# The down product of the prompt's rows as seven block products, with sums of w_down made by GpSimd during the gates

## The chip, the core and the metric

The kernel runs on one core of a Trainium2 chip. A core has five engines with an instruction stream each: TensorE (PE, matrix products), VectorE (DVE), ScalarE (ACT), GpSimd (POOL) and SyncE (SP, which here only issues transfers). They meet through semaphores. Transfers go through 16 DMA engines that all streams share. The metric is device time in microseconds; the kernel before took 1920.28 us, the median of 3 runs (1920.12 to 1924.04).

## The reference, cut to what matters

The reference is one layer of a decoder for 1024 prompt rows and 64 sample rows (8 sequences with 8 new tokens each), so 1088 rows of width 1024, in float32.

```
z = rmsnorm(x, norm1_g) @ w_in            # 1024 -> 5120: queries, keys, values (3072) and two gates (2048)
gate = sigmoid(g + b_gate)                # 16 tiles of 128 channels, "the gates"
m = gate[0] * (o_a @ w_proj_a) + gate[1] * (o_b @ w_proj_b)
x = x + m @ w_o
u = rmsnorm(x, norm2_g) @ w_up            # 1024 -> 5632, then a causal convolution of width 3
f = gelu(a) * b                           # a, b: the two halves, 2816 channels each = 22 tiles of 128
y = rmsnorm(x + f @ w_down, norm_f_g)     # the down product: 2816 -> 1024
```

Outputs are y for all rows and the new key, value and convolution caches; most of the cache output is a shifted copy of an input (`cache3` is 8 x 4 MB).

## The kernel before

All large products are float32 products made of three passes: each operand is split into a head (its value rounded to the multiplier's format, made by ACT) and a rest (made by DVE), and TensorE adds head x head, head x rest and rest x head.

The work is in stages, one after the other, with the order of each engine written out by hand; no planner decides anything. Only semaphores tie the engines, and each engine takes its own list strictly in order. Three stages are touched.

The front stage (`front_stage`, up to about 490 us) makes z in six column blocks of 512, and then the gates, in 8 units of two channel tiles. A unit is a Strassen-Winograd product: four block products' worth of matrices are combined so that seven block products P1 to P7 of 24 matmuls (128x272 each) do instead of eight. Its weights arrive by `load_unit` (line 330, 1 MB, issued by POOL) in one of two buffers `raw_g0`, `raw_g1`; ACT makes the heads (`unit_head`, line 415), DVE the rests (`unit_rest`, line 598) and the four sums S1 to S4 of the weights. `load_unit(s)` waits until every rest of unit s - 2 is made (`lo_made`). POOL also issues `copy_cache` (line 333), eight copies of 4 MB from HBM to HBM: four of them beside the loads of z's blocks, one right after `load_unit(0)`, three in the gates.

The tail stage (`tail_stage`, from about 997 us) makes m, x and then u: three channel tiles plainly and 19 in units like those of the gates (from 1233 to 1635 us). There the four weight sums of a unit are made by POOL (`sum_s3`, `sum_s2`, `sum_s1`, `sum_s4`, lines 2369, 2374, 2380, 2385), which also stores each finished tile of f to HBM (`store`, line 2389). The convolution runs on DVE (lines 2728 and 2733).

The down product (from 1635 us) goes through the nine row tiles in three trios (`TRIOS`). Each trio takes 22 steps, one for each channel tile k: SP loads 128 rows of w_down (512 KB) and the trio's part of f (192 KB), ACT and DVE split both, and PE does `down(n)`, 18 matmuls of 128x512 (16 in the last trio, whose sample tile needs fewer). Two buffers of each kind are in use, so a step's load can be at most two steps ahead. As step 4 is reached, x (4.3 MB) is loaded back (lines 2350 and 2351). Finished banks are added to x by DVE (`add_out`, lines 2784 and 2786), followed by the square, the root and the scaling (`scale_out`, line 2798) of the final norm, and SP stores y.

## Time and profile before

| | |
|---|---|
| time, median of 3 | 1920.28 us |
| the profiled execution | 1921.66 us, its span 1920.0 us |
| PE busy | 1787.1 us (93%), 12290 matmuls |
| DVE, ACT, POOL busy | 1131.9, 794.1, 251.3 us |
| granted TensorE clock, mean | 0.966 of full speed |
| the down product's matmuls (line 3070) | 1144, 263.4 us busy |
| HBM traffic | 283 MB read, 96 MB written |

How to read it: the profile is one execution. An engine's busy time says little by itself, since each stage has another limit; what counts is in which stretches PE stands still or runs at a lower clock, and what it waits for there. The rows below are from the windows (busy time by stretch), the timelines of single engines (start, duration, what ended the idle time before), the groups of instructions and the list of transfers.

### The profile page before, as it was taken

To read this page: it belongs to the slowest core of one execution; us is meant where nothing else is said; L and a number is where in the kernel's file an instruction comes from. 1 tells how busy PE (TensorE), PEld (TensorE's weight loads), DVE (VectorE), ACT (ScalarE), POOL (GpSimd) and SP (SyncE) were. 2 spreads that over 40 slices of the span, in tenths; PEclk is the share of its full clock that TensorE was granted. 3 is DMA by queue.
4 is the path that set the end of the run, shared out by engine and by line. 5 is a ranking of instruction groups with operands and counts; after the bars stand their busy time and mean duration, and the time that the engine had idled before them with its cause. 6 is when DMAs were issued, how large, how long until landed. Compare 5 with 4: busy or idle time off the path is not lost. (4 is left out here: it accounts for less than half of the span.)

```text
span 1920.0 us, 32200 instructions
## 1 busy us (share of the span) xinstructions
PE 1787.1 (93%) x12290; PEld 1526.8 (80%) x12290; DVE 1131.9 (59%) x1935; ACT 794.1 (41%) x1479; POOL 251.3 (13%) x321
## 2 busy tenths in 40 slices
PE   7999999899778887999988999999999999899997
PEld 6777779899545555666668889999999999788875
DVE  5224575343364787666667368667777776445455
ACT  4220014343673576333332134455555554334343
POOL 0000000000100301232300002133223222000000
PEclk9999999999978789999989999999999999999998
DMA  6444535732711936999956435132232222756664
GB/s 232 173 178 178 215 121 183 263 111 72 194 29 42 323 120 229 392 386 389 385 187 216 148 116 180 48 90 68 68 95 75 68 70 86 249 177 203 190 209 139
DMA packets 169826, 331.13 MB, mean 172 GB/s; under 512 B 35769, under 2 KB 97098, under 8 KB 167306
## 3 DMA queue, kind: packets, MB, share of 16 engines
q1 hardware_dynamic: 143242, 193.58, 30.8%
q0 software_dynamic: 26432, 135.50, 19.4%
q8 instruction: 98, 1.61, 0.3%
q14 instruction: 54, 0.44, 0.1%
HBM read 283.02 MB, written 95.68 MB: 197 GB/s over the span
## 5 line engine op out<-in xcount | busy, mean ns | idle before, releaser
L3070 PE MATMUL tl_ps<-tl_dn,tl_f 128*128 128x512 f32 x1144 | 263.4, 392 | 8.5 <-DVE tl_f L2771 6.9
L3070 PEld LDWEIGHTS tl_ps<-tl_dn,tl_f 128*128 128x128 f32 x1144 | 216.1, 189 | 55.5 <-DVE tl_dn L2767 8.9
L3004 PE MATMUL tl_ps<-tl_T_hi,tl_slots 128*128 128x272 f32 x1216 | 211.5, 288 | 1.2 <-ACT tl_u L2456 1.2
L3004 PEld LDWEIGHTS tl_ps<-tl_T_hi,tl_slots 128*128 128x128 f32 x1216 | 175.4, 188 | 1.5 <-ACT tl_u L2456 1.5
L3004 PE MATMUL tl_ps<-tl_X_hi,tl_slots 128*128 128x272 f32 x912 | 161.1, 288 | 0.7 <-ACT tl_u L2525 0.7
L2767 DVE TENSOR_TENSOR tl_dn<-all_lead,tl_dn 128x1024 fp32r<-128x1024 f32 x66 | 80.9, 1225 | 136.5 <-ACT tl_dn L2534 136.5
L766 PE MATMUL fr_ps<-fr_w_hi,h_hi 128*128 128x512 f32 x384 | 152.7, 398 | 2.4 <-DVE h_lo L550 2.4
L766 PE MATMUL fr_ps<-fr_w_lo,h_hi 128*128 128x512 f32 x384 | 152.1, 396 | 0.0
L766 PE MATMUL fr_ps<-fr_w_hi,h_lo 128*128 128x512 f32 x384 | 150.3, 391 | 0.0
L2534 ACT ACTIVATE tl_dn<-all_lead 128x1024 fp32r<-128x1024 f32 x66 | 70.0, 1060 | 160.4 <-PE tl_ps L3070 132.7
L3004 PEld LDWEIGHTS tl_ps<-tl_X_hi,tl_slots 128*128 128x128 f32 x912 | 132.2, 188 | 0.9 <-ACT tl_u L2525 0.9
L2728 DVE SCALAR_TENSOR_TENSOR tl_c<-tl_u,tl_cw,tl_c 128x1023 f32<-128x1023 f32 x88 | 121.2, 1378 | 15.1 <-ACT tl_c L2473 13.5
L3004 PE MATMUL tl_ps<-tl_T_lo,tl_slots 128*128 128x272 f32 x608 | 125.5, 288 | 0.0
L3004 PEld LDWEIGHTS tl_ps<-tl_T_lo,tl_slots 128*128 128x128 f32 x608 | 95.8, 189 | 0.0
L3004 PE MATMUL tl_ps<-tl_X_lo,tl_slots 128*128 128x272 f32 x456 | 94.1, 288 | 0.0
L766 PEld LDWEIGHTS fr_ps<-fr_w_hi,h_hi 128*128 128x128 f32 x384 | 72.6, 189 | 21.1 <-DVE h_lo L550 2.8
L766 PEld LDWEIGHTS fr_ps<-fr_w_hi,h_lo 128*128 128x128 f32 x384 | 72.7, 189 | 16.2
L766 PEld LDWEIGHTS fr_ps<-fr_w_lo,h_hi 128*128 128x128 f32 x384 | 72.8, 190 | 14.4
L778 PE MATMUL fr_ps<-h_hi,fr_slots 128*128 128x272 f32 x480 | 83.0, 287 | 0.0
L778 PE MATMUL fr_ps<-fr_X_hi,fr_slots 128*128 128x272 f32 x384 | 69.1, 292 | 8.0 <-DVE fr_slots L598 7.3
L2473 ACT ACTIVATE tl_c<-tl_u,tl_cb,tl_cw 128x1088 f32<-128x1088 f32 x44 | 57.1, 1298 | 47.0 <-DVE tl_u L2756 46.2
L2743 DVE TENSOR_TENSOR tl_slots<-all_lead,tl_slots 128x512 fp32r<-128x512 f32 x70 | 62.4, 904 | 23.5 <-ACT tl_slots L2505 23.1
(384 smaller groups left out, 3734.4 us busy)
## 6 DMA issues: line engine op xcount, KB each, us to landing
all_lead<-in_w_down SPq DMA_DIRECT2D x66, 512.0 KB, 3.6
out_s<-in_cache POOLq DMA_DIRECT2D x8, 4080.0 KB, 20.6
pg_pages<-in_pool POOLq DMA_DIRECT2D x64, 256.0 KB, 6.3
pg_pages<-in_pool SPq DMA_DIRECT2D x64, 256.0 KB, 7.2
pg_odds<-in_pool SPq DMA_DIRECT2D x64, 256.0 KB, 7.9
all_lead<-in_w_up SPq DMA_DIRECT2D x26, 512.0 KB, 5.1
zs<-fr_zt SPq DMA_DIRECT2D x48, 256.0 KB, 2.0
fd<-tl_c POOLq DMA_DIRECT2D x22, 544.0 KB, 4.9
```

The costliest lines, as they stand in the source:

```text
L766: last = pe.matmul(zbank[at % 3], h[:, k, c0:c0 + P], w[:, k, :], start=(m == 0), stop=(m == 3 * KD - 1))
L778: last = pe.matmul(ps[:, (bank + n) * 512:(bank + n) * 512 + SIDE // 2], w[:, k, :], h[:, k, n * SIDE // 2:(n + 1) * SIDE // 2], start=(fi ...
L2473: act.activation(c[:, i, :], row, ACT.Identity, bias=cb[:, t:t + 1], scale=cw[:, 2, t:t + 1]).then_inc(scaled, 1)
L2534: act.activation(dn[n % 2][:, 0, :], dn_raw[:, n % 2, :], ACT.Copy).then_inc(dn_hi_done, 1)
L2728: dve.scalar_tensor_tensor(out=x, in0=row[:, p0:p1 - back_by], scalar=cw[:, tap_of, t:t + 1], in1=x, op0=ALU.mult, op1=ALU.add).then_inc(t ...
L2743: dve.tensor_tensor(slots[:, SLOT_OF[name], 1, :, :], weights(s_, name), slots[:, SLOT_OF[name], 0, :, :].bitcast(F32), ALU.subtract).then ...
L2767: dve.tensor_tensor(x[:, 1, :], dn_raw[:, n % 2, :], x[:, 0, :].bitcast(F32), ALU.subtract).then_inc(dn_lo_done, 1)
L3004: last = pe.matmul(ps[:, (bank + n) * 512:(bank + n) * 512 + SIDE // 2], w[:, k, :], h[:, k, n * SIDE // 2:(n + 1) * SIDE // 2], start=(fi ...
L3070: last = pe.matmul(down_bank(m), x, w[:, h * 512:h * 512 + 512], start=(k == 0 and q == 0), stop=(k == FT - 1 and q == len(passes) - 1), s ...
```

## The change

Three edits, in two stages.

First, the down product of the 1024 prompt rows becomes a Strassen-Winograd product. The 22 channel tiles are halved into 11 and 11, the rows into 512 and 512, and the 1024 output columns into 512 and 512. Seven products P1, P6, P2, P5, P3, P7, P4 come one after the other (`DOWN`), each over 11 channel tiles (`FH`), with 4 row tiles times 3 passes = 12 matmuls of 128x512 in a step. A step now loads two pieces of 256 KB: a block of f or of its sums (`sd`), and a block of w_down or of its sums (`td`). Raw steps go through 4 buffers and split steps through a ring of 11. The 64 sample rows are multiplied plainly beside P1, P2, P5 and P3 (two matmuls for each channel tile and column half). In the last product the four row tiles are finished one after the other (`last_down`), each followed by its own norm and store.

Second, the sums. POOL makes those of w_down in the front stage: 22 parts, each with two loads, four additions of 128x256 and a store to `td`, with two buffers. They stand in POOL's list between the `load_unit` calls, four parts ahead of each of units 3 to 7. POOL makes the sums of f in the tail stage as the tiles are finished (`difference`, `add_sums`). The weight sums of the 19 units, which POOL made before, move to DVE.

Third, `copy_cache`: all eight copies are now issued beside the loads of z's blocks, two for each of blocks 2 to 5; none is left in the gates.

```diff
@@ front_stage, POOL @@
                 load(p)
-                copy_cache(p - 2)
-            pool.wait_ge(xn_ready, RT)
+                copy_cache(2 * p - 4)
+                pool.wait_ge(z_ready, (p - 1) * RT + 5)
+                copy_cache(2 * p - 3)
             load_unit(0)
-            copy_cache(NZ - 2)
...
             load_unit(1)
-            copy_cache(NZ - 1)
-            for s_ in range(2, NU):
-                pool.wait_ge(lo_made, 7 * (s_ - 1))
-                load_unit(s_)
-                if s_ < 4:
-                    copy_cache(NZ - 2 + s_)
+            def load_part(i):
+                if i >= 2:
+                    pool.wait_ge(wsum_stored[i % 2], 16 * (i // 2))
+                for q in range(2):
+                    pool.dma_start(wsum[:, i % 2, q, :, :], w_parts[i // 2, i % 2, q]).then_inc(wsum_in[i % 2], 16)
+            def sum_part(i):
+                x = wsum[:, i % 2, :, :, :]
+                pool.wait_ge(wsum_in[i % 2], 32 * (i // 2 + 1))
+                pool.tensor_tensor(x[:, 1, 1, :], x[:, 1, 1, :], x[:, 0, 1, :], ALU.subtract).then_inc(wsum_step, 1)
...
+                pool.wait_ge(wsum_step, 4 * i + 4)
+                pool.dma_start(td[i // 2, :, :, (i % 2) * 256:(i % 2) * 256 + 256],
+                               x.rearrange("p q n c -> p (q n) c")).then_inc(wsum_stored[i % 2], 16)
+            pool.wait_ge(lo_made, 7)
+            load_unit(2)
+            pool.wait_ge(t_lo_done, 3)
+            load_part(0)
+            for i in range(2 * FH):
+                if i + 1 < 2 * FH:
+                    load_part(i + 1)
+                sum_part(i)
+                if i % 4 == 3 and 3 + i // 4 < NU:
+                    pool.wait_ge(lo_made, 7 * (2 + i // 4))
+                    load_unit(3 + i // 4)
@@ tail_stage @@
+        DOWN = ("P1", "P6", "P2", "P5", "P3", "P7", "P4")
+        STEPS = len(DOWN) * FH
+        LEAD = 5
...
@@ SP @@
             for n in range(STEPS):
                 if n == 4:
+                    sp.wait_ge(tap, 8 * (FT - 1))
+                    sp.wait_ge(beside, 8 * (FT - 1))
+                    load_samples(0)
                     sp.wait_ge(p_ready, made("P3", UNITS - 1, UNITS))
                     sp.dma_start(x2[:, 0:QT, :], ...).then_inc(x2_back, 16)
...
@@ POOL, for each tile j of f from the 12th on @@
+            def add_sums(j):
...
+                pool.tensor_tensor(sums[:, 0, :], c[:, 1, HALF2], sums[:, 0, :], ALU.subtract).then_inc(sum_step, 1)
+                pool.tensor_tensor(sums[:, 1, :], c[:, 1, HALF2], sums[:, 1, :], ALU.add).then_inc(sum_step, 1)
...
+                pool.tensor_tensor(s4[:, :], c[:, 1, HALF1], sums[:, 0, :], ALU.subtract).then_inc(sum_step, 1)
@@ DVE, units and down product @@
                     rest(s_ + 1, "S3")
+                    sum_s2(s_ + 1)
                     rest(s_ + 1, "S2")
+                    sum_s1(s_ + 1)
                     rest(s_ + 1, "S1")
+                    sum_s4(s_ + 1)
...
+                q, after = divmod(n - FH - LEAD, FH)
+                if q >= 0 and after == 0:
+                    for at in range(4):
...
+                                add_out(DOWN[q], at, quarter)
...
+            for at in range(4):
+                add_out("P4", at, (1, 0))
+                finish(1 + at)
@@ PE @@
+            def row_tile(n, q, r):
+                k, (hi, lo) = n % FH, (ring[n % FH][:, part, :] for part in range(2))
+                for m, (x, w) in enumerate(three_passes(hi[:, r * P:r * P + P], lo[:, r * P:r * P + P], hi[:, 512:1024], lo[:, 512:1024])):
+                    last = pe.matmul(down_bank(4 * q + r), x, w, start=(k == 0 and m == 0), stop=(k == FH - 1 and m == 2))
...
+            def last_down():
+                q = len(DOWN) - 1
+                for r in range(4):
+                    bank_free(4 * q + r)
+                    for k in range(FH):
+                        if r == 0:
+                            pe.wait_ge(step_lo, q * FH + k + 1)
+                        row_tile(q * FH + k, q, r)
```

POOL's list in the gates, before: loads of units (`fr_raw_g`) and copies (`out_s3`), each load behind DVE's rests.

```order
L330 DMA fr_raw_g1<-in_w_in 128x8x256 [waits fr_z_stored1,fr_z_stored2,fr_z_stored0,fr_z_ready]
L333 DMA out_s3<-in_cache3 64x16320
L330 DMA fr_raw_g0<-in_w_in 128x8x256 [waits fr_lo_made]
L333 DMA out_s3<-in_cache3 64x16320
L330 DMA fr_raw_g1<-in_w_in 128x8x256 [waits fr_lo_made]
```

The same place in the changed kernel, from one part's loads to the next unit's load; three more such parts stand between the load of unit 2 and this one, and four between any two later unit loads.

```order
L362 DMA fr_wsum<-in_w_down 128x2x256 [waits fr_wsum_stored0]
L362 DMA fr_wsum<-in_w_down 128x2x256
L368 TENSOR_TENSOR fr_wsum<-fr_wsum 128x256 [waits fr_wsum_in1]
L370 TENSOR_TENSOR fr_wsum<-fr_wsum 128x256 [waits fr_wsum_step]
L372 TENSOR_TENSOR fr_wsum<-fr_wsum 128x256 [waits fr_wsum_step]
L374 TENSOR_TENSOR fr_wsum<-fr_wsum 128x256 [waits fr_wsum_step]
L376 DMA td<-fr_wsum 512x1x256 [waits fr_wsum_step]
L334 DMA fr_raw_g1<-in_w_in 128x8x256 [waits fr_lo_made]
```

The copies have gone from here, and a unit's load now stands behind additions and behind waits for stores of the sums.

DVE's list in one unit of the tail, before: rests (`tl_slots`) and the first half of the convolution.

```order
L2762 TENSOR_TENSOR tl_u1<-tl_u1,tl_ps 128x544
L2743 TENSOR_TENSOR tl_slots<-tl_raw1,tl_slots 128x512 x4
L2728 SCALAR_TENSOR_TENSOR tl_c<-tl_u1,tl_cw,tl_c 128x1023
L2733 SCALAR_TENSOR_TENSOR tl_c<-tl_ue,tl_cw,tl_c 128x2x32
L2728 SCALAR_TENSOR_TENSOR tl_c<-tl_u1,tl_cw,tl_c 128x1022
```

The same unit in the changed kernel, with the sums (`tl_raw1<-tl_raw1`) between the rests.

```order
L2885 TENSOR_TENSOR tl_u1<-tl_u1,tl_ps 128x544
L2845 TENSOR_TENSOR tl_slots<-tl_raw1,tl_slots 128x512 x2
L2856 TENSOR_TENSOR tl_raw1<-tl_raw1 128x4x128
L2845 TENSOR_TENSOR tl_slots<-tl_raw1,tl_slots 128x512
L2862 TENSOR_TENSOR tl_raw1<-tl_raw1 128x4x128
L2845 TENSOR_TENSOR tl_slots<-tl_raw1,tl_slots 128x512
L2867 TENSOR_TENSOR tl_raw1<-tl_raw1 128x4x128
L2830 SCALAR_TENSOR_TENSOR tl_c<-tl_u1,tl_cw,tl_c 128x1023
```

The rests and the convolution keep their order; three sums stand among them, and the fourth (`sum_s3`) ahead of the unit's last product.

## Rows read from the trace of the kernel before

**Rows 1.** Windows: stretch; busy PE, PEld, DVE, ACT, POOL; clock, DMA share, GB/s
```profile
100.00:200.00 100.00, 100.00 (x469) 80.04 (x468) 38.84 (x59) 13.53 (x8) 2.86 (x4) 1.00 0.47 173
340.00:360.00 20.00, 18.94 (x152) 18.73 (x151) 3.24 (x6) 2.29 (x4) 1.14 (x2) 1.00 0.96 352
360.00:380.00 20.00, 13.79 (x97) 13.82 (x98) 8.61 (x14) 8.32 (x13) 0.90 (x1) 0.83 0.53 172
1300.00:1400.00 100.00, 100.00 (x799) 100.00 (x799) 73.42 (x93) 51.34 (x101) 27.73 (x22) 1.00 0.27 82
1650.00:1660.00 10.00, 3.10 (x10) 2.26 (x9) 2.26 (x3) 3.05 (x4) 0.00 (x0) 0.83 0.82 274
```

**Rows 2.** Timeline of POOL in the gates: start, duration, instruction, idle before
```profile
322.84 0.90 POOL L330 DMA_DIRECT2D fr_raw_g<-in_w_in  x1 [7.23 <-DVE fr_slots L598]
...
339.71 0.90 POOL L330 DMA_DIRECT2D fr_raw_g<-in_w_in  x1 [15.45 <-DVE fr_slots L598]
...
371.90 0.90 POOL L330 DMA_DIRECT2D fr_raw_g<-in_w_in  x1 [30.75 <-DVE fr_slots L598]
...
411.71 0.88 POOL L330 DMA_DIRECT2D fr_raw_g<-in_w_in  x1 [20.07 <-DVE fr_slots L598]
432.67 0.88 POOL L330 DMA_DIRECT2D fr_raw_g<-in_w_in  x1 [20.07 <-DVE fr_slots L598]
```

**Rows 3.** Timeline of ACT in the gates
```profile
364.20 0.62 ACT L423 ACTIVATE fr_even_u<-fr_ps 128x544 f32<-128x544 f32 x1 [15.50 <-DMA gs<-fr_even_u]
...
388.11 0.61 ACT L415 ACTIVATE fr_slots<-fr_raw_g 128x512 fp32r<-128x512 f32 x1
392.08 0.63 ACT L427 ACTIVATE held_rows<-fr_ps 128x544 f32<-128x544 f32 x1 [3.36 <-PE fr_ps L778]
...
454.94 0.63 ACT L427 ACTIVATE fr_even_u<-fr_ps 128x544 f32<-128x544 f32 x1 [3.35 <-PE fr_ps L778]
```

**Rows 4.** Groups on POOL: instruction, shapes, count; busy us, mean ns; idle before
```profile
L2385 POOL TENSOR_TENSOR all_lead<-all_lead 128x512 f32<-128x512 f32 x10 | 17.4, 1737 | 0.0
...
L2374 POOL TENSOR_TENSOR all_lead<-all_lead 128x512 f32<-128x512 f32 x10 | 12.8, 1279 | 34.7 <-DVE tl_slots L2743 34.7
...
L952 POOL DMA_DIRECT2D pd_krow<-zs x7 | 5.0, 723 | 69.3 <-POOLq L141 59.9 <-PE pd_tbank L1134 9.3
```

**Rows 5.** Transfers issued by POOL: count, KB each, median us to landing
```profile
out_s<-in_cache POOLq DMA_DIRECT2D x8, 4080.0 KB, 20.6
...
fd<-tl_c POOLq DMA_DIRECT2D x22, 544.0 KB, 4.9
...
fr_raw_g<-in_w_in POOLq DMA_DIRECT2D x8, 1024.0 KB, 7.1
...
x2d<-tl_x POOLq DMA_DIRECT2D x8, 512.0 KB, 2.9
```

**Rows 6.** Group: the matmuls of the down product
```profile
L3070 PE MATMUL tl_ps<-tl_dn,tl_f 128*128 128x512 f32 x1144 | 263.4, 392 | 8.5 <-DVE tl_f L2771 6.9 <-DVE tl_f L2774 0.8 <-DVE tl_x L2786 0.6
```

**Rows 7.** Timeline of all engines, last trio of the down product and the end
```profile
1887.91 0.33 SPq L2298 DMA_DIRECT2D all_lead<-in_w_down  x1
...
1891.54 0.33 SPq L2298 DMA_DIRECT2D all_lead<-in_w_down  x1
...
1903.57 0.69 DVE L2784 TENSOR_TENSOR tl_x<-tl_x,tl_ps 64x512 f32<-64x512 f32 x1 [1.23 <-PE tl_ps L3070]
...
1914.09 1.28 DVE L2798 SCALAR_TENSOR_TENSOR tl_y<-tl_x,tl_rstd,tl_gain_f 128x1024 f32<-128x1024 f32 x1
```

**Rows 8.** The chain that ended last, start of the down product: start, us, what
```profile
1642.42 14.51 DMA tl_f_raw<-fd
```

**Rows 9.** Timeline of DVE in one unit of the tail
```profile
1417.96 0.72 DVE L2762 TENSOR_TENSOR tl_u<-tl_u,tl_ps 128x544 f32<-128x544 f32 x1 [2.53 <-ACT tl_u L2525]
1418.60 1.29 DVE L2743 TENSOR_TENSOR tl_slots<-tl_raw,tl_slots 128x512 fp32r<-128x512 f32 x2
1422.00 1.17 DVE L2743 TENSOR_TENSOR tl_slots<-tl_raw,tl_slots 128x512 fp32r<-128x512 f32 x1 [2.11 <-ACT tl_slots L2505]
```

More of the change, by code:

```diff
@@ L55 @@
 UNITS = FT - PLAIN_UP
+FH = FT // 2
 def rows_of(t):
@@ L2122, in _, with tail_stage @@
             turn_out_shared(NB - 1)
-def tail_stage(nc, K, a, o, zs, gs, early, x2d, fd):
+def tail_stage(nc, K, a, o, zs, gs, early, x2d, fd, sd, td):
     with stage(nc, "tl") as s:
@@ L2229, in bank_pair, with sample_bank, added_before @@
+        def sample_bank(i):
+            return ps[:, S_BANKS[i] * 512:S_BANKS[i] * 512 + 512]
+        def added_before(name, r, quarter):
+            before = [ADDED[what] for what in ADDS[:ADDED[(name, r, quarter)] - 1] if what[1:] == (r, quarter)]
+            return max(before, default=0)
         def bank_pair(b):
@@ new lines, in load_step, with load_samples @@
+                if name in ("P1", "P2", "P3"):
+                    r0, c0 = (0 if name == "P1" else FH) + k, 512 if name == "P3" else 0
+                    sp.dma_start(to[:, 512:1024], a["w_down"][r0 * P:r0 * P + P, c0:c0 + 512]).then_inc(landed, 16)
+                else:
+                    sp.dma_start(to[:, 512:1024], td[k, :, ("P6", "P5", "P4", "P7").index(name), :]).then_inc(landed, 16)
+            def load_samples(i):
+                for s_ in range(2):
+                    c0 = s_ * (ROWS - SROWS // 2)
+                    sp.dma_start(fs_raw[:, :, s_ * SROWS // 2:(s_ + 1) * SROWS // 2],
+                                 fd[i * FH:(i + 1) * FH, :, c0:c0 + SROWS // 2].rearrange("k p r -> p k r")).then_inc(fs_in, 16)
@@ L2633, in _ @@
             for n in range(4, STEPS):
[L2634 to L2639 removed]
+                step_head(n)
+                if n == 4:
+                    sample_heads(0)
+                if n == FH + 3:
+                    sample_heads(1)
+                if n == FH + LEAD:
+                    for at in range(4):
+                        keep(at)
+                if 0 <= n - 5 * FH - LEAD - 1 < FIRST:
+                    final_square(n - 5 * FH - LEAD - 1)
+                if n == 5 * FH + LEAD + 7:
+                    final_root(0)
+            for g in range(1, len(NORMS)):
                 for i in range(*NORMS[g]):
@@ L2888, in _ @@
             rest(1, "A11")
+            sum_s3(1)
             for s_ in range(UNITS):
@@ new lines, in row_tile, with samples_part @@
+            def row_tile(n, q, r):
+                k, (hi, lo) = n % FH, (ring[n % FH][:, part, :] for part in range(2))
+                for m, (x, w) in enumerate(three_passes(hi[:, r * P:r * P + P], lo[:, r * P:r * P + P], hi[:, 512:1024], lo[:, 512:1024])):
+                    last = pe.matmul(down_bank(4 * q + r), x, w, start=(k == 0 and m == 0), stop=(k == FH - 1 and m == 2))
+                if k == FH - 1:
+                    last.then_inc(out_ready, 1)
+                return last
+            def samples_part(n, half, side, first, final):
+                k, (hi, lo) = n % FH, (ring[n % FH][:, part, 512:1024] for part in range(2))
+                pe.wait_ge(fs_lo_done, half + 1)
+                for m, w in enumerate((hi, lo)):
+                    last = pe.matmul(sample_bank(side), fs[half][:, k, :], w, start=(first and k == 0 and m == 0),
+                                     stop=(final and k == FH - 1 and m == 1))
+                if final and k == FH - 1:
+                    last.then_inc(s_ready, 1)
+                return last
@@ new lines, in first_samples, with down @@
+            def first_samples(k):
+                if k == 0:
+                    pe.wait_ge(c21_done, UNITS)
+                samples_part(k, 0, 0, True, False)
+                samples_part(k, 0, 1, True, False).then_inc(d_done, 1)
+            def down(q):
+                name = DOWN[q]
+                for k in range(FH):
+                    n = q * FH + k
+                    pe.wait_ge(step_lo, n + 1)
+                    if name == "P2":
+                        samples_part(n, 1, 0, False, True)
+                    if name == "P5":
+                        samples_part(n, 0, 1, False, False)
+                    if name == "P3":
+                        samples_part(n, 1, 1, False, True)
+                    for r in range(4):
+                        if k == 0:
+                            bank_free(4 * q + r)
+                        last = row_tile(n, q, r)
+                    if q and k < FH - 1:
+                        last.then_inc(d_done, 1)
+                    if q == 0 and k >= 4:
+                        first_samples(k - 4)
+                if q == 0:
+                    for k in range(FH - 4, FH):
+                        first_samples(k)
@@ L3116, in _ @@
                     p7(s_ + 1)
-            for n in range(STEPS):
-                down(n)
+            for q in range(len(DOWN) - 1):
+                down(q)
+            last_down()
 def program(nc, a, o, scratch):
```

411 lines of the change are left out of this document (232 added, 179 removed).

## The prediction

> **What bounds the kernel now.** I read the windows first, stretch by stretch, because the three edits lie in three stages. In the blocks of z, PE is busy for the whole stretch although one 4 MB copy runs beside each block: 100 of 100 us, DMA share 0.47 [rows 1]. In the units of the tail PE is again busy for 100 of 100 us, while DVE stands at 73 and POOL at 28 [rows 1]. So z and the units are bound by PE, and there an edit on another engine only matters if it comes to the path. Two stretches are not like that. From 340 to 380 us PE is busy for 32.7 of 40 us, and in the second half its granted clock is 0.83 [rows 1]. The timeline of POOL shows the same place: unit loads, which otherwise follow each other at 20.96 us (432.67 - 411.71), are 32.2 us apart there (371.90 - 339.71) [rows 2]. ACT tells why: it stood 15.5 us for a store of the gates that was late [rows 3], while the copies of the cache, 20.6 us each [rows 5], held the DMA engines (share 0.96). That stall costs 11.2 us, of which 7.3 are idle and 3.9 are work at the lower clock. The second place is the start of the down product: 3.1 of 10 us busy at 1650 us [rows 1]. There a step's load took 14.5 us behind the 4.3 MB of x [rows 8]. Elsewhere the down product is PE-bound: 8.5 us idle before 1144 matmuls [rows 6], and 16 matmuls every 3.63 us in the last trio, 0.227 us each [rows 7].
>
> **The down product.** The new one has 7 x 11 x 12 = 924 matmuls for the prompt and 4 x 11 x 2 = 88 for the samples, 1012 in place of 1144, all 128x512. 132 fewer at 0.227 us are **-30.0 us**. Feeding them is not the limit: a step is 12 matmuls, 2.7 us, and needs one head and one rest of 128x1024 and 512 KB, and the ring reaches 11 steps ahead where two buffers did before. Three places are left.
>
> At the start the load of x stands again ahead of step 4's load in SP's list. x and step 4 land about where x and step 4's load landed before (14.5 us after issue, [rows 8]); head and rest take some 2.3 us more, so step 4 is ready near 1655 us. The four steps ready by then are 10.9 us of work instead of 16.3, with step 3 late by some 2 us behind the convolution. That makes some 9.5 us of idle where before had 8.5 [rows 6]: **+1**. It could be +6 if the 2816 small pieces of the sample rows are slow, and 0 at best.
>
> At the last product all 11 steps are wanted within the first row tile, one each 0.68 us. DVE makes the rests of five of them only after the eight additions for P7, at about 0.7 us each, that it stands in at P7's end. The eleventh is ready about 9.7 us after that end, where PE wants it after 6.8: **+2.9**. Bounds 0 and 6. For the changes of banks at the other products I take **+1**: PE has 6 matmuls of the next product, 1.4 us, before it needs a bank that DVE has just freed.
>
> At the end, 17.7 us lie between PE's last matmul (1903.57 - 1.23) and the end of the span [rows 7]. Six additions of 0.69 us become one, and two scalings of 1.28 us and a square leave the chain, because each row tile is now finished by itself while PE is at the next: **-7** (bounds -4 and -9).
>
> The down product in sum: -30 + 1 + 2.9 + 1 - 7 = **-32 us**.
>
> **The units.** Four sums of 128x512 come to DVE, at the 0.645 us that a rest takes in quiet [rows 9]: 2.6 us of a 21 us unit. Two things cover them. DVE stands 2.5 us before its first subtraction and 2.1 us before a rest, where it waits for ACT's head of a sum that POOL took 1.28 us for [rows 4, 9]; DVE makes that sum in half the time, so the chain S2, head, rest, S1, head, rest gets no longer. And the rest in [rows 9] that took 1.17 us beside POOL's additions would take 0.65 alone. I take **0**; if the cover fails, DVE is late by up to 1 us a unit, 19 us in all, and the sums of f on POOL (three additions of 128x512 a tile) are far from filling 21 us.
>
> **The copies.** Moved beside z's blocks they run one at a time, half a block apart. The stretch of 100 us in [rows 1] held two loads and two copies (the 4 instructions on POOL) with PE at 100 of 100; it will hold four copies of 20.6 us each [rows 5], 82 of 100 us. I take 0 there. In the gates the stall of 11.2 us goes. What is late next is not PE but POOL.
>
> **The sums of w_down.** Here the change adds waits to the list that feeds the gates. In a part, POOL waits for the store of the part before (only two buffers, and that store was issued just ahead), issues two loads, makes four additions, each behind the one before, and issues the next store. So the landing of the store lies bare in every part. The period:
> - store from issue to landing: 2.9 us for 512 KB of x2d when all is quiet, 4.9 for 544 KB of fd beside loads [rows 5]. The new one goes out in pieces of 1 KB, beside the gates' stores; I take 3.4, nearer to the size and the quiet.
> - two load issues at 0.72 us: 1.4 [rows 4].
> - four additions of 128x256: half of 1.28 (quiet) to half of 1.74 (beside DVE) [rows 4]; I take 0.75, which makes 3.0. No row has the short form.
> - semaphores between them, 0.3.
>
> That is **8.1 us a part**, bounds 7.2 (2.9 + 1.4 + 2.6 + 0.3) and 10.1 (4.9 + 1.4 + 3.5 + 0.3). Four parts stand ahead of each unit's load: 32 us, where PE takes 20.96 us a unit. Queued behind the waiting part is the unit's load, and ACT waits for it: the head of a unit's A11 (L415 at 388.11) stands in ACT's list ahead of `keep_u2` (L427 at 392.08, 3.4 us after ACT fell idle [rows 3]), and PE's P7 waits for that one. So unit 7's weights must have landed by 454.94 - 0.63 = 454.3 us to cost nothing. They land as follows. Unit 2's load goes at 322.84 [rows 2] and takes 7.1 us [rows 5]; part 0 lands behind it, near 331.3. The 20th part ends 19 periods, four additions (3.3) and a store issue (0.7) later, and the load takes 7.1 us more: 331.3 + 19 x 8.1 + 11.1 = 496.3 us. Late by **42 us**, net of the stall that goes, since 454.3 is measured with that stall in it. After each wait PE starts at a lower clock, as it did after 360 us; before the last wait this hides in the next one, but the 30 us of PE work after it pay once: **+4**.
>
> In the Trainium skill, "GPSIMD Engine Reference", the section on elementwise work side by side, gives 2.6 cycles an element for a two-input addition at 1.2 GHz, 0.56 us for 256 elements, and calls VectorE the place for such work. The trace shows more, 1.28 us for 512 in quiet. By the page the period is 7.3 us and the total comes out near zero; that is the edge of the first rival below, and I keep the row. "DMA: Bandwidth & Descriptors", rules for kernel authors, says to issue a transfer early and wait for it late so that its fixed cost is covered; this loop does it for its loads and not for its stores. With the stores covered the period would be 5.4 us (1.4 + 3.0 + 0.3 and 0.7 for the store's issue) and POOL would all but keep up, near the second rival's time.
>
> **Sum.** 0 (z) + 42 + 4 (gates) + 0 (units) - 32 (down product) = +14 on the profiled execution's 1921.66 us, 1935.7. The median of the runs is 1.4 us below that execution, so I forecast **1934 us**.
>
> **Rivals.**
> 1. The sums' period is short enough, and the kernel is faster. The place is POOL's loop in the gates, the point at which it decides is 19P - 111.9 + 4 - 32 = 0, P = 7.36 us. For it: 7.2 is a bound made of rows, with the store at the 2.9 us of x2d. Against it: it needs both the quiet store and the quiet additions, and the gates have their own stores and DVE's work beside them. At 6.9 us the time is 1911.
> 2. POOL keeps up entirely (period 5.0 or less): the gates lose their 11.2 us and the down product its 32: 1877. Against it, every row puts the bare landing of a store at 2.9 us or more, and the rest alone makes more than 5.0.
> 3. The period is long, 9.5 us or more: the landing at 4.9 as for fd, and both engines slowed by each other. 19 x 9.5 - 111.9 + 4 - 32 = +41, 1961.
> 4. DVE becomes the bound of the units: +1 us each, 1953. For it, DVE goes from 73 to over 80 of 100; against it, the 2.5 us in which it stands at the turn of the units.
> 5. The change does not do what it says in the down product: steps come late because DVE stands in additions while rests are due, and only half of the 32 us comes: 1950.
>
> **How the numbers follow.** Chances: forecast 0.52, rival 1 0.19, rival 2 0.03, rival 3 0.13, rival 4 0.06, rival 5 0.07. A difference under 0.2% (3.8 us) can't be told from none in this kernel. Faster by more takes rival 2 and most of rival 1, 0.19; within 0.2% takes the rest of rival 1 and the low flank of the forecast (P from 7.2 to 7.6), 0.11; slower is the rest, 0.70. The range goes from 1908 (P near 6.8, or 7.2 with a down product better by 8) to 1964 (P near 9.7), which leaves out rival 2 and the upper part of rival 3.
>
> **What would show it.** In the gates: POOL's loads of units 4 to 7 about 32 us apart instead of 20.96, the last one near 489 us; ACT waiting for DMA ahead of L415's line of A11; PE idle for some 11 us in each unit from 4 on; POOL's additions of 128x256 at 0.65 to 0.87 us; the store to td at 2.9 to 4.9 us. The late store of the gates near 350 us gone. In the units: 21 us a unit and PE at 100 of 100. In the down product: 1012 matmuls, about 242 us from first to last, one idle stretch of 8 to 9 us in P1 and one of 3 us in the first row tile of P4; some 10.5 us after the last matmul. I am wrong if the unit loads come less than 29 us apart, or if the stretch from the first down matmul to the end is not 28 to 36 us shorter than before.

## The result, and the profile after

The changed kernel takes **1974.25 us** (median of 4, 1972.01 to 1977.93) beside 1920.2 us for the kernel before on the same chip: ratio 1.0274, 95% interval 1.0252 to 1.0297. It is slower, as forecast, but by 54 us and not by 14, and outside the range of 1908 to 1964. The profiled execution has a span of 1976.3 us, 56.3 more than before, at a mean clock of 0.953. Medians here are of fast runs alone; one run of e11_spread_x2, 2496.48 us at a clock of 0.648, is left out for that.

Where the 56 us lie is read from the first and last start of PE's matmuls in each stage (us from the start of the span):

| | before | after | difference |
|---|---|---|---|
| last matmul of the gates | 488.6 | 555.2 | +66.6 |
| first matmul of the tail's units | 1233.3 | 1302.2 | +68.9 |
| first matmul of the down product | 1634.8 | 1713.2 | units: 401.5 to 411.0, **+9.5** |
| last start of a down matmul | 1906.3 | 1965.9 | 271.5 to 252.7, **-18.8** |
| end of the span | 1920.0 | 1976.3 | 13.7 to 10.4, **-3.3** |

68.9 + 9.5 - 18.8 - 3.3 = 56.3. Of the 68.9, 66.6 are in the gates and 2.3 in the stages behind them, which the change leaves alone. The busy times and counts of the page after:

```profile
PE 1775.6 (90%) x12180; PEld 1514.3 (77%) x12180; DVE 1198.4 (61%) x1974; ACT 777.0 (39%) x1431; POOL 354.3 (18%) x514
```

First the windows of the kernel after, with the columns of [rows 1]:

```profile
100.00:200.00 100.00, 100.00 (x469) 80.03 (x469) 38.56 (x59) 13.55 (x8) 4.39 (x7) 1.00 0.74 265
340.00:360.00 20.00, 20.00 (x163) 20.00 (x162) 11.10 (x14) 8.04 (x12) 13.02 (x17) 1.00 0.49 158
400.00:420.00 20.00, 6.45 (x37) 6.45 (x38) 2.00 (x4) 2.51 (x5) 13.65 (x19) 0.57 0.53 176
1600.00:1700.00 100.00, 94.72 (x746) 93.62 (x745) 88.24 (x104) 47.58 (x98) 30.64 (x42) 1.00 0.40 131
1730.00:1740.00 10.00, 2.82 (x7) 2.25 (x8) 2.13 (x3) 2.91 (x4) 2.14 (x5) 0.58 1.04 386
```

z carries twice the copies (DMA share 0.74 for 0.47 in [rows 1]) and PE loses nothing. The old stall near 350 us is gone. In its place PE stands two thirds of the time at 400 us; it loses 5 of 100 us in the late units. The start of the down product is as poor as before: 2.82 of 10 us busy, where [rows 1] have 3.10.

POOL's timeline in the gates, which answers to [rows 2]:

```profile
323.11 0.88 POOL L334 DMA_DIRECT2D fr_raw_g<-in_w_in  x1 [7.73 <-DVE fr_slots L633]
...
340.31 1.11 POOL L368 TENSOR_TENSOR fr_wsum<-fr_wsum 128x256 f32<-128x256 f32 x1
...
344.49 0.76 POOL L376 DMA_DIRECT2D td<-fr_wsum  x1 [0.30 <-POOL fr_wsum L374]
348.13 1.41 POOL L362 DMA_DIRECT2D fr_wsum<-in_w_down  x2 [2.89 <-DMA td<-fr_wsum]
349.57 0.74 POOL L368 TENSOR_TENSOR fr_wsum<-fr_wsum 128x256 f32<-128x256 f32 x1
...
363.28 0.97 POOL L334 DMA_DIRECT2D fr_raw_g<-in_w_in  x1
370.56 1.42 POOL L362 DMA_DIRECT2D fr_wsum<-in_w_down  x2 [6.30 <-DMA td<-fr_wsum]
...
405.39 0.98 POOL L334 DMA_DIRECT2D fr_raw_g<-in_w_in  x1
442.15 0.97 POOL L334 DMA_DIRECT2D fr_raw_g<-in_w_in  x1
477.40 0.98 POOL L334 DMA_DIRECT2D fr_raw_g<-in_w_in  x1
513.95 0.98 POOL L334 DMA_DIRECT2D fr_raw_g<-in_w_in  x1
```

One part can be read off: additions and the signal behind them 4.18 us (340.31 to 344.49), the store until the next load may go 3.64, two load issues 1.44; the period is 9.26 us. The one long wait, 6.30 in place of 2.89 us, stands behind unit 3's load (363.28), where two loads of SP (issued at 360.18) and the unit's own 1 MB were under way and the DMA share from 362 to 371 us was 0.98. Behind the four later unit loads the wait is 2.08 us at most, which with the unit load's own issue of 0.98 is hardly more than 2.89, so these cost next to nothing. From the first addition of one part to that of the next, the mean of the 19 periods up to unit 7's load is 9.4 us: 3.97 until the store is issued, 4.02 until the next load may go, 1.44 for the load issues. So unit loads go out 35 to 42 us apart, where PE needs one every 20.96. The waits of ACT and POOL in the gates (total, times, longest), and a group on POOL (busy us, mean ns), say the same:

```profile
ACT fr_slots L450 <- DMA fr_raw_g<-in_w_in: 90.5, 5, 20.4
POOL fr_wsum L362 <- DMA td<-fr_wsum: 60.1, 20, 6.3
```
```profile
L368 POOL TENSOR_TENSOR fr_wsum<-fr_wsum 128x256 f32<-128x256 f32 x22 | 18.3, 832 | 4.3 <-DMA fr_wsum<-in_w_down 3.9
```

In a late unit of the tail DVE and POOL run like this (two timelines of the same stretch); DVE's row answers to the two rests of 1.29 us in [rows 9]:

```profile
1662.65 0.71 DVE L2885 TENSOR_TENSOR tl_u<-tl_u,tl_ps 128x544 f32<-128x544 f32 x1
1663.28 5.24 DVE L2845 TENSOR_TENSOR tl_slots<-tl_raw,tl_slots 128x512 fp32r<-128x512 f32 x2
```
```profile
1663.59 1.30 POOL L2468 TENSOR_TENSOR tl_sums<-tl_c,tl_sums 128x512 f32<-128x512 f32 x1
1664.84 1.29 POOL L2469 TENSOR_TENSOR tl_sums<-tl_c,tl_sums 128x512 f32<-128x512 f32 x1
1666.09 1.28 POOL L2471 TENSOR_TENSOR tl_s<-tl_c,tl_sums 128x512 f32<-128x512 f32 x1
```

The row merges two rests, 5.24 us for 1.29 before. A narrower window shows the first alone:

```profile
1663.28 4.64 DVE L2845 TENSOR_TENSOR tl_slots<-tl_raw,tl_slots 128x512 fp32r<-128x512 f32 x1
```

One rest took 4.64 us, the next 0.68. POOL's three additions beside it last 3.78 us and run close to their quiet speed (1279 ns in [rows 4]). PE's groups (busy us, mean ns, idle before and for whom) show what that does to the units, and the counts of the down product, beside [rows 6]:

```profile
L3158 PE MATMUL tl_ps<-tl_T_hi,tl_slots 128*128 128x272 f32 x1216 | 212.2, 289 | 8.8 <-DVE tl_u L2879 7.6 <-ACT tl_u L2539 1.2
...
L3217 PE MATMUL tl_ps<-tl_ring_t 128*128 128x512 f32 x672 | 162.4, 394 | 13.0 <-DVE tl_ring_t L2889 13.0
...
L3217 PE MATMUL tl_ps<-tl_ring_a 128*128 128x512 f32 x252 | 60.1, 390 | 0.9 <-DVE tl_ring_a L2889 0.9
...
L3227 PE MATMUL tl_ps<-tl_ring_t,tl_fs 128*128 128x512 f32 x80 | 22.7, 389 | 0.0
...
L3227 PE MATMUL tl_ps<-tl_ring_a,tl_fs 128*128 128x512 f32 x30 | 8.8, 389 | 0.0
```

The sample rows take 80 + 30 = 110 matmuls, not 88. The start of the down product in the chain that ended last, beside [rows 8], and PE's own row there:

```profile
1716.15 18.64 DMA tl_raw<-in_w_down
...
1734.81 1.06 ACT tl_ring_t L2618
```
```profile
1737.18 5.20 PE L3217 MATMUL tl_ps<-tl_ring_t 128*128 128x512 f32 x12 [9.82 <-DVE tl_ring_t L2889]
```

### The profile page after: what moved, and what is told of

Its sections match the earlier page's. It is cut to its first block and busy times, and to the rows that moved or that the text cites. A ratio compares the mean times of both kernels' runs of the same rounds, so it can differ in the third digit from the quotient of the medians.

```text
span 1976.3 us, 32216 instructions
## 1 busy us (share of the span) xinstructions
PE 1775.6 (90%) x12180; PEld 1514.3 (77%) x12180; DVE 1198.4 (61%) x1974; ACT 777.0 (39%) x1431; POOL 354.3 (18%) x514
## 5 line engine op out<-in xcount | busy, mean ns | idle before, releaser
L3217 PE MATMUL tl_ps<-tl_ring_t 128*128 128x512 f32 x672 | 162.4, 394 | 13.0 <-DVE tl_ring_t L2889 13.0
L3217 PEld LDWEIGHTS tl_ps<-tl_ring_t 128*128 128x128 f32 x672 | 127.2, 190 | 42.3 <-DVE tl_ring_t L2889 16.0
L813 PE MATMUL fr_ps<-fr_X_hi,fr_slots 128*128 128x272 f32 x384 | 75.8, 314 | 64.3 <-ACT fr_even_u L462 36.5
L2830 DVE SCALAR_TENSOR_TENSOR tl_c<-tl_u,tl_cw,tl_c 128x1023 f32<-128x1023 f32 x88 | 112.9, 1283 | 16.5 <-ACT tl_c L2557 14.9
L813 PEld LDWEIGHTS fr_ps<-fr_X_hi,fr_slots 128*128 128x128 f32 x384 | 62.7, 212 | 65.7 <-ACT fr_even_u L462 37.2
L633 DVE TENSOR_TENSOR fr_slots<-fr_raw_g,fr_slots 128x512 fp32r<-128x512 f32 x54 | 43.8, 826 | 109.8 <-ACT fr_slots L450 109.8
L801 PEld LDWEIGHTS fr_ps<-fr_w_lo,h_hi 128*128 128x128 f32 x384 | 72.8, 190 | 14.4
L1785 DVE COPY pg_kt<-sm_tbank 128x512 f32<-128x512 f32 x92 | 58.3, 651 | 30.0 <-PE sm_tbank L2015 29.3
```

Source lines behind the costliest of these rows:

```text
L633: dve.tensor_tensor(split_slot(s_, name, 1), weights(s_, name), split_slot(s_, name, 0).bitcast(F32), ALU.subtract).then_inc(lo_made, 1)
L801: last = pe.matmul(zbank[at % 3], h[:, k, c0:c0 + P], w[:, k, :], start=(m == 0), stop=(m == 3 * KD - 1))
L813: last = pe.matmul(ps[:, (bank + n) * 512:(bank + n) * 512 + SIDE // 2], w[:, k, :], h[:, k, n * SIDE // 2:(n + 1) * SIDE // 2], start=(fi ...
L1785: eng.tensor_copy(dst, src).then_inc(moved[1], 1)
L2830: dve.scalar_tensor_tensor(out=x, in0=row[:, p0:p1 - back_by], scalar=cw[:, tap_of, t:t + 1], in1=x, op0=ALU.mult, op1=ALU.add).then_inc(t ...
L3217: last = pe.matmul(down_bank(4 * q + r), x, w, start=(k == 0 and m == 0), stop=(k == FH - 1 and m == 2))
```

## The experiments

Stage lengths come from one profile each, as in the table above. The stages between the gates and the units, which no kernel here changes, took 738 to 752 us in the profiles (with one exception, e3_unitloads); so a difference of a few us is read from the stage it belongs to, and the total only from the medians. The runs were made on several chips, on which the kernel before took between 1920.2 and 1924.55 us in the median; each ratio is to the kernel before on the same chip, so totals of different experiments are compared by their ratios. Six kernels with the same down product (the kernel after, e2, e3, e4, e8, e9) took 252.0 to 253.5 us from its first to its last matmul, which is the spread to set beside a difference there.

**e1_copies** (the kernel before with the third edit alone)

```diff
-                copy_cache(p - 2)
+                copy_cache(2 * p - 4)
+                pool.wait_ge(z_ready, (p - 1) * RT + 5)
+                copy_cache(2 * p - 3)
...
-                if s_ < 4:
-                    copy_cache(NZ - 2 + s_)
```

> The kernel before, with the cache copies of group 3 moved beside the z products and nothing else of the change. Theory C (the copies delayed a unit's load in the gates, and beside z they cost nothing): the stretch with PE half idle near 350 us goes, the last matmul of the gates starts about 11 us earlier than 488.6 us, the total is 1920 - 11 = 1909 us. Rival (they cost z what they give the gates): PE below 100 of 100 us in 100:200, and the total stays at 1920 us within 4.

Measured: 1912.44 us, ratio 0.9951 (0.9936 to 0.9967). Gates end at 479.8 us, 8.8 earlier where 11 were expected, PE at 100 of 100 us in 100:200. Theory C holds: the copies are free beside z.

**e2_third** (a third buffer for the parts, in space free at that time)

```diff
-                if i >= 2:
-                    pool.wait_ge(wsum_stored[i % 2], 16 * (i // 2))
+                if i >= 3:
+                    pool.wait_ge(wsum_stored[i % 3], 16 * (i // 3))
...
-                if i + 1 < 2 * FH:
-                    load_part(i + 1)
+                if i + 2 < 2 * FH:
+                    load_part(i + 2)
                 sum_part(i)
```

> The kernel after, with a third buffer for the w_down parts, so that a part's load no longer waits for the store just issued. Theory P (the part's period of 9.3 us is a serial loop on POOL: store's landing, loads' landing, additions): the period falls to POOL's own issues and additions, about 6.5 us; unit loads come 4 x 6.5 = 26 us apart, still more than a unit's 21 us, the gates end about 50 us earlier than 555 us, the total is 1974 - 50 = 1924 us (1915 to 1935). Rival Q (POOL's additions and issues alone make the 9.3 us): period over 8.5 us, total above 1955 us.

Measured: 1977.9 us, ratio 1.0276 (1.0249 to 1.0302): nothing gained, a miss. Its timeline on POOL:

```profile
344.28 0.76 POOL L377 DMA_DIRECT2D td<-fr_wsum  x1 [0.30 <-POOL fr_wsum L375]
347.92 1.41 POOL L363 DMA_DIRECT2D fr_wsum<-in_w_down  x2 [2.89 <-DMA td<-fr_wsum]
```

The load looks one part further ahead, and so with three buffers it needs again the one whose store was issued just before. What counts is the number of buffers less the lookahead, counted from the part whose additions come next: 2 - 1 in the kernel after, 3 - 2 here. e8_third_after makes it 3 - 1.

**e3_unitloads** (units 2 to 7 loaded by SP)

```diff
+                    if i and s_ + 2 < NU:
+                        sp.wait_ge(lo_made, 7 * (s_ + 1))
+                        load_unit(sp, s_ + 2)
                     sp.wait_ge(g_done, 2 * s_ + i + 1)
...
-                if i % 4 == 3 and 3 + i // 4 < NU:
-                    pool.wait_ge(lo_made, 7 * (2 + i // 4))
-                    load_unit(3 + i // 4)
```

> The kernel after, with the gates' unit loads from the third unit on issued by SP between its two stores of a unit; POOL keeps only the w_down parts. Theory P (POOL's total sets the end of the stage too, since the next stage begins when all engines are done): PE runs the units in about 21 us each and ends near 480 us, then waits for POOL, whose 22 parts of 9.2 us end near 540 us; total 1974 - 15 = 1959 us (1945 to 1970). Rival O (only the order on POOL's queue costs, unit loads behind parts): the stage ends near 480 us, total 1974 - 75 = 1899 us.

Measured: 1968.56 us, ratio 1.0238 (1.0217 to 1.0259). PE's last matmul of the gates starts at 497.3 us, 58 earlier than in the kernel after, and then, from the waits of PE:

```profile
PE pd_tbank L1169 <- PEq L142: 57.9, 1, 57.9
```

PE stands 57.9 us at the stage's end, while POOL issues its last store at 548.43 us. Rival O falls: the parts cost twice, once through the unit loads behind them and once through their own end. (497 and not 480: ACT still waited 44.7 us for unit loads, since SP issued each one unit later than its buffer allowed. e9_gates, which issues them earlier, has no such wait.)

**e8_third_after** (three buffers, the load behind the additions)

```diff
-                if i + 1 < 2 * FH:
-                    load_part(i + 1)
                 sum_part(i)
+                if i + 2 < 2 * FH:
+                    load_part(i + 2)
```

> As e2_third, but a part's load is issued behind the next part's additions, so that the store it waits for was issued one part earlier and not just now. Theory P (e2_third gained nothing because its load still waited 2.9 us for the store issued 0.8 us before): the wait of 2.9 us on td<-fr_wsum goes, the period falls from 9.3 us to two load issues 1.4, four additions 3.6 to 4.6, 0.3 and one store issue 0.8, together 6.1 to 7.1 us; unit loads 25 to 30 us apart; the gates end 40 to 55 us earlier than 555 us; total 1974 - 47 = 1927 us (1919 to 1936). Rival Q (DMA traffic sets the period, whatever the buffers): total within 8 us of 1974 us.

Measured: 1923.37 us, ratio 1.0013 (0.9999 to 1.0027); gates end at 504.5 us, 50.7 earlier. POOL:

```profile
341.06 0.76 POOL L377 DMA_DIRECT2D td<-fr_wsum  x1 [0.30 <-POOL fr_wsum L375]
341.73 1.41 POOL L363 DMA_DIRECT2D fr_wsum<-in_w_down  x2
343.17 0.74 POOL L369 TENSOR_TENSOR fr_room_raw<-fr_room_raw 128x256 f32<-128x256 f32 x1
```

The wait is gone, 5.6 to 7.5 us from store to store, and unit loads 25 to 28 us apart from unit 3's on. Theory P holds; one line moved behind another is worth 49 us of the gates between e2_third (553.9) and this. Whether two buffers would do with the load behind the additions was not tested.

**e4_dve_parts** and **e9_gates** (the additions by DVE, 0.42 to 0.43 us each; POOL only issues; unit loads by SP; e9_gates with both orders mended)

```diff
-                pool.tensor_tensor(x[:, 1, 1, :], x[:, 1, 1, :], x[:, 0, 1, :], ALU.subtract).then_inc(wsum_step, 1)
...
+                    dve.tensor_tensor(x[:, 1, 1, :], x[:, 1, 1, :], x[:, 0, 1, :], ALU.subtract).then_inc(wsum_step, 1)
...
# e9_gates against e4_dve_parts
-                        load_unit(sp, s_ + 2)
+                        load_unit(sp, s_ + 3)
...
-                if i + 2 < 2 * FH:
-                    load_part(i + 2)
                 store_part(i)
+                if i + 2 < 2 * FH:
+                    load_part(i + 2)
```

> The kernel after, with the w_down parts' additions done by DVE (three parts for each unit of the gates), three buffers, POOL only issuing their loads and stores, and unit loads on SP. Theory P: nothing in the gates is late any more, 88 additions of about 0.4 us fit into DVE's idle 60%; the gates end near 480 us, total about 1974 - 75 = 1899 us. Rival D (an addition on DVE ahead of a rest or of a finished quarter delays PE): units of 22 to 24 us, gates end 490 to 505 us, total 1909 to 1924 us.

> e4_dve_parts with two orders mended: SP issues a unit's load one unit earlier (as soon as its buffer is split, behind the first of its two stores), and POOL stores a part before it loads the next but one. Theory P (what was left in e4_dve_parts, 15 us of PE waiting for keeps and loads, came from these loads one unit late, and DVE's 88 additions cost PE nothing): gates end near 480 us in place of 500, total 1918 - 18 = 1900 us (1895 to 1905). Rival D (DVE's additions delay PE): at least 8 us of the 15 stay, total 1908 us or more.

Measured: e4_dve_parts 1917.68 us, ratio 0.9974 (0.9959 to 0.9988), gates end at 500.8; e9_gates 1909.18 us, ratio 0.9928 (0.9909 to 0.9947), gates end at 487.4. Both intervals lie below 1, and e9_gates is 0.7% faster than the kernel before. The sizes were too hopeful by 19 and 9 us. e4_dve_parts lands in rival D's range (gates 490 to 505 us), but PE's 15 us of waiting there are for ACT, which waited 32.8 us for unit loads: with both orders mended and the additions left where they are the gates end 13.4 us earlier, so the late loads were the larger part. In e9_gates PE waits 5.6 us up to the gates' end and some 8 us against e1_copies stay. Its median falls to rival D, though 2 of the 9 us are the chip (the kernel before took 1924.55 there and 1922.53 beside e4_dve_parts, from which the 1900 was worked out); e12_even_parts asks what is left. The three edits (third buffer, additions on DVE, unit loads on SP) stand together here; their shares were not tested.

**e12_even_parts** asked what costs the last us of the gates (on top of e10_all, below):

```diff
-                    sum_parts(2 if s_ in (1, 2) else 1)
+                    if s_:
+                        sum_parts(1)
...
-                    sum_parts(1)
+                    sum_parts(4 if s_ == NU - 2 else 1)
```

> e10_all with the w_down parts spread evenly over DVE's program in the gates: one in the first unit, three in each of the next five, six in the seventh, in place of up to four in a unit. Theory L (the gates' last 6 us against e1_copies, 486 for 480 us, are DVE standing up to 8.0 us for a part's load ahead of rests that PE needs): gates end 481 to 483 us, total 1882.5 - 4 = 1878 us (1875 to 1881). Rival D (the additions themselves, 88 of 0.43 us, cost it): gates end at 486 us, total within 1.5 us of 1882.5 us.

Measured: 1886.26 us, ratio 0.9806 (0.9787 to 0.9826), not faster than e10_all; gates end at 491.3 us. A miss in size, but PE's waits from 330 to 490 us tell the cause apart:

```profile
PE fr_ps L827 <- DVE held_rows L667: 8.0, 1, 8.0
PE fr_ps L827 <- DVE held_rows L661: 1.3, 1, 1.3
```

In the units with three parts PE waits 1.3 us in all; the one with six costs 8.0, where DVE stands 3.3, 1.5, 4.5 and 0.8 us for loads that are still on their way. The standing costs, as theory L says, and I had only moved it. The additions by themselves, twelve for each of the five units with three parts, left PE that one wait of 1.3 us, which speaks against rival D.

**e5_dve_sums** (the three f sums of tiles 11 to 21 by DVE)

```diff
-                pool.tensor_tensor(sums[:, 0, :], c[:, 1, HALF2], sums[:, 0, :], ALU.subtract).then_inc(sum_step, 1)
...
                 product(j)
+                if j >= FH:
+                    add_sums(j)
```

> The kernel after, with the three additions per channel tile from tile 11 on made by DVE behind the product and not by POOL. Theory S (while POOL adds two rows of SBUF, DVE's additions stand still for all of POOL's 3.9 us): three additions of 512 columns cost DVE about 0.6 us each, 1.8 in place of 3.96 us, DVE has 18.4 of 21.07 us busy before, so a unit comes back to about 21.1 us, and the total falls by up to 9.5 us, to 1965 us (1963 to 1968). Rival V (DVE is the bound of a unit and each us on it counts): the period is 22.4 - 3.96 + 1.8 with waits, over 21.8 us, total 1970 us or more.

Measured: 1962.59 us, ratio 1.0221 (1.0202 to 1.024), 0.53% or 10 us under the kernel after. The units take 401.5 us, to a tenth what they took before the change. DVE's timeline:

```profile
1644.80 0.69 DVE L2842 TENSOR_TENSOR tl_sums<-tl_c,tl_sums 128x512 f32<-128x512 f32 x1
...
1647.69 1.28 DVE L2849 TENSOR_TENSOR tl_slots<-tl_raw,tl_slots 128x512 fp32r<-128x512 f32 x2
```

Three additions of 0.69 us are on DVE and the two rests are back at 1.28. Theory S holds: DVE was not too full, it was held. The Trainium skill, "SBUF — State Buffer", under "SBUF: two separate sides", says that of a VectorE instruction with two SBUF inputs and a GpSimd instruction that reads SBUF, whichever starts first has the shared pair of ports for its whole length, while the other is blocked. The rows agree that one engine waits out the other. They do not show that the first to start has the ports: in the kernel after, the rest's record begins 0.31 us before that of GpSimd's first addition (1663.28 and 1663.59) and ends 0.56 us behind the third (1667.92 and 1667.37).

**e6_late_x2** and **e11_spread_x2** (the 4 MB of x later, and then in pieces)

```diff
+                if n == 8:
                     sp.wait_ge(p_ready, made("P3", UNITS - 1, UNITS))
                     sp.dma_start(x2[:, 0:QT, :], x2d[0:SEQ, :].rearrange("(t p) d -> p t d", p=P)).then_inc(x2_back, 16)
# e11_spread_x2, behind load_step(n)
+                if 8 <= n <= 24 and n % 2 == 0:
+                    t = (n - 8) // 2
...
+                    sp.dma_start(x2[0:rows, t, :], x2d[t * P:t * P + rows, :]).then_inc(x2_back if t < 4 else x2_rest, 16)
```

> The kernel after, with the 4 MB load of x2 moved from ahead of the fifth step's load to ahead of the ninth's, and DVE's wait for it moved to the first addition. Theory X (step 4's data queue behind x2's 4 MB: PE idle 9.82 us, clock 0.58 in 1730:1740): the 9.8 us and 1 to 2 us of slow clock go, total 1974 - 10 = 1964 us (1961 to 1967), unless the steps behind it are late by as much. Rival Y (the load collides with whatever steps stand behind it): a stall of the same size at steps 8 to 10, total within 3 us of 1974 us.

> The kernel after, with the 4 MB of x2 loaded one row tile of 512 KB behind each even step's load from step 8 to 24, not in one piece. Theory Y (one transfer of 4 MB holds up the steps' loads behind it wherever it stands, as at steps 8 to 10 in e6_late_x2, where ACT waited 20.3 us): in pieces each delays a step by 1 to 2 us, which the ring's lead covers; PE's 9.8 us before step 4 go, total 1974 - 9 = 1965 us (1962 to 1969). Rival W (the steps' traffic of 0.5 MB each is itself the bound at the start, so that any further byte costs): total 1970 us or more.

Measured: e6_late_x2 1973.98 us, ratio 1.0278 (1.0259 to 1.0296), no gain; rival Y. Step 4 is on time, and the wait stands at step 8, on ACT and then on PE:

```profile
1746.78 1.06 ACT L2619 ACTIVATE tl_ring_t<-tl_raw 128x1024 fp32r<-128x1024 f32 x1 [20.28 <-DMA tl_raw<-in_w_down]
```
```profile
1749.15 3.36 PE L3219 MATMUL tl_ps<-tl_ring_t 128*128 128x512 f32 x7 [9.61 <-DVE tl_ring_t L2890]
```

e11_spread_x2: 1968.15 us, ratio 1.0225 (1.0203 to 1.0247), down matmuls 247.2 us for 252.7. The 9.8 us of idle are gone, but 2.9 come back where PE waits for a bank that DVE's first additions free:

```profile
1762.84 8.69 PE L3224 MATMUL tl_ps<-tl_ring_a 128*128 128x512 f32 x30 [2.90 <-DVE tl_x L2914]
```

DVE is not idle ahead of these additions (1762.11 us); they stand in its list behind seven rests from 1751.24 us on, before which DVE stood 7.6 us for steps whose loads were late, at a DMA share of 1.05 from 1740 to 1760 us. The gain is 5.5 us of the 9 expected. The total lies in theory Y's range and under rival W's, but the share shows that the traffic which rival W names is close by.

**e7_rests_first** (P7's additions behind the rests of P4)

```diff
-                if q >= 0 and after == 0:
+                if q >= 0 and after == (5 if q == 5 else 0):
```

> The kernel after, with DVE's rests of the last five steps of P4 ahead of its eight additions of P7. Theory R (P4's first row tile waits for rests that stand behind the additions, PE 18.26 of 20 us in 1930:1950): 1.5 to 2 us less, total 1972 us. Rival N (P7's additions then come late for P4's third row tile's bank, or P4's own wait shortens only to be given back at the end): no change within 1 us.

Measured: 1973.23 us, ratio 1.028 (1.0258 to 1.0302). The median cannot tell it from the kernel after. In the profile PE's four waits in P4's first row tile, 1.74 us in all with the longest 1.24, are gone, and the down matmuls take 249.6 us for 252.7, which is below the 252.0 to 253.5 of the kernels with the same down product. So theory R is right in the place, and the 1.74 us fit its 1.5 to 2.

**e10_all** (e9_gates, the f sums on DVE, x in pieces, P4's rests first; the edits are those above)

> e9_gates together with the sums of f on DVE (e5_dve_sums), x2 loaded row tile by row tile behind steps 8 to 24 (e11_spread_x2) and P4's rests first (e7_rests_first). If the prices add up: 1900 - 11 (sums of f) - 8 (x2) - 1 = 1880 us (1873 to 1888), 40 us under the kernel before. If they overlap (DVE's late rests at the start of the down product hide behind the x2 stall), 1888 us or more.

Measured: **1882.54 us, ratio 0.9792 (0.9772 to 0.9813)**, 2.1% under the kernel before. The expectation of 1880 holds, though its parts came out otherwise: e9_gates, from which it starts, took 9 us more than the 1900 assumed, and the down product gained 14.4 us where 9 were assumed. Its down matmuls take 238.3 us, against 252.7 in the kernel after, while the single edits gave 5.5 (e11), 3.1 (e7) and 1.8 (e5), together 10.4. So 4 us come only with the edits together. Most of it stands at one place: the wait of 2.90 us that e11_spread_x2 alone had before DVE's first additions is 0.32 us here, and the `tl_ring_a` matmuls behind it take 390 ns in the mean and not 404 (the clock in e11_spread_x2 was 0.83 from 1760 to 1770 us). DVE reaches those additions 44.0 us after the first down matmul, and 46.9 us in e11_spread_x2; which other edit makes it earlier, no run shows. PE's idle time there:

```profile
L3243 PE MATMUL tl_ps<-tl_ring_t 128*128 128x512 f32 x672 | 159.1, 390 | 2.6 <-DVE tl_ring_t L2910 2.6
```

## Why the prediction was right and wrong

The bound, the mechanism and the sign were right in the gates: the bare landing of a store in POOL's serial loop, with the unit loads queued behind it. Three terms were off, all to one side (20.6 + 9.5 + 9.9 = 40.0 us), and make the 40 us between 1934 and 1974. The profiled executions differ by 2.3 more (1935.7 and 1977.93), which lie in stages that the change leaves alone. Of the prediction's own two signs of being wrong one came: unit loads were 35 to 42 us apart, not less than 29, but the stretch from the first down matmul to the end is 22.1 us shorter and not 28 to 36.

**The period of a part, +21 us.** The prediction took 8.1 us. Measured in the mean of 19 periods: additions with their gaps and signal 3.97 where it had 3.3 (832 ns each, not 750: the row beside DVE would have been the nearer one), the store until the next load 4.02 where it had 3.4 (its landing has a median of 3.4 us, as forecast; with the step to the next load it is 3.6 to 3.7 in sixteen periods, but 7.95, 4.96 and 4.40 in three, which had no term), the load issues 1.44 where it had 1.4. From the first addition of part 0 at 330.7 us to unit 7's load it makes (513.95 - 4.2 - 330.7) / 19 = 9.42 us. The prediction's own formula with it is 19 x 9.42 - 111.9 = +67; the gates ended 66.6 later. The term for the clock (+4) was not needed, and so the 25 us of the longer period come out as 21. e8_third_after shows the mechanism by taking it away. Rival 3 has nearly this period (9.5 us), but by another way: it needs the landing at 4.9 us, and the median is 3.4. The Trainium skill's rule in "DMA: Bandwidth & Descriptors", rules for kernel authors (wait late), was read rightly, and e2_third shows that a buffer alone does not follow it.

**The units, +9.5 us, where the step took 0.** I had weighed the four sums that come to DVE and their cover, and that part held: with them on DVE, units take 401.5 us in e5_dve_sums. The failed step is the clause that the sums of f "are far from filling 21 us". POOL had the room, but it is DVE that pays for them: one rest beside them took 4.64 us, and PE waits for what comes after it. The sign was in [rows 9], a rest of 1.17 in place of 0.65 us beside POOL; I read it as something that the change takes away and not as what it brings back threefold. Rival 4 has the right symptom with the wrong cause: DVE was late in the late units, but with the sums of f on it too (e5_dve_sums) it is not.

**The down product, -22 for -32.** Two misreadings. The samples are multiplied five times, not four (P1's columns serve both halves), so 1034 matmuls: the page's totals are 12290 before and 12180 after, 110 fewer and not 132, which is -25.0 us at 0.227. And the end: 17.7 us were measured from the addition at 1903.57 [rows 7], which is that of the first tile of the trio, while PE's last matmul starts at 1906.3. From there the end went from 13.7 to 10.4 us, -3.3 and not -7; the 10.5 us forecast behind the last matmul were right. The stalls came to +6.2 (-18.8 + 25.0) where the terms +1, +2.9 and +1 had 4.9, with another split: in the first 80 us from its start PE did 287 matmuls where before it did 312, which is some 5.7 us for the +1; P4's first row tile cost 1.7 for the 2.9, and the changes of banks nothing. (The kernel before lost 1.6 us of its own behind the first 80.) The start is dearer because step 4's load landed 18.6 us after its issue, where the row before had 14.5 [rows 8]; ACT and PE stood 10.7 and 9.8 us for it. Why it took longer is not shown; the DMA share from 1730 to 1740 us was 1.04, where the stall before had 0.82.

**What held.** The copies are free beside z and give the gates 8.8 us (e1_copies). The late store near 350 us is gone. What is late next is POOL, which decides the sign.

## What to carry to other kernels

A loop with N buffers that loads L parts ahead of the part it works on next waits for the store issued N - L parts back, and at 1 that is the one just issued: count that, and not the buffers. Before work goes to an idle GpSimd, look what VectorE does at that moment: in this kernel two-input additions on the one held those on the other (a rest of 0.68 us took 4.64), and the same additions may be cheaper on the busy engine (three of 0.69 us in place of a hold of almost 4). And work that is queued ahead of a stage's loads costs twice if it also outlasts the stage (PE stood 57.9 us for it in e3_unitloads).

## What the runs showed that I had not expected

Three GpSimd additions of 1.3 us in a row held one VectorE rest of 0.68 us until 0.56 us after the last of them, with no turn for VectorE between them, while GpSimd lost nothing. The trace of the kernel after has nine such chains with a unit's rest in them, and it is so in each; in seven the rest begins 0.31 us before the chain and takes 4.64 or 4.65 us. In the gates both engines lost: GpSimd's 44 additions of 128x256 with no VectorE work beside them took 0.72 to 0.74 us each, the others up to 1.30, and VectorE's of 128x512 took 0.69 alone and up to 1.66 beside them. One transfer of 4 MB held up the 256 KB loads issued behind it wherever it stood: in the kernel after the first of them landed 18.6 us after its issue, and in e6_late_x2 ACT waited 20.3 us for one. Why the untouched middle stages vary from 738 to 752 us between profiles stays open; no run was made for it.
